# The retention gate's sigmoid, written with ScalarE's exponential and two VectorE operations

## What is computed

```python
h = rms_norm(x, g_mix[l])
proj = h @ w_in[l]
rq, rk, rv, rg, sq, sk, sv, mq = jnp.split(proj, split_at, axis=-1)
...
scores = jnp.einsum('bnihd,bnjhd->bnhij', qc, kc) * intra
...
o = o * lax.rsqrt(jnp.mean(o * o, axis=-1, keepdims=True) + EPS)
o = jax.nn.silu(g.astype(f32)) * o
...
x = x + jnp.concatenate([o_ret, o_swa, o_mem], axis=-1) @ w_out[l]
x = x + moe_ffn(rms_norm(x, g_ffn[l]), ...)
```

## Time and profile before

| | us |
|---|---|
| median of 3 runs | 1069.91 |
| lowest, highest | 1068.23, 1070.17 |
| the profiled execution | 1068.5 |
| its span, first to last instruction | 1066.7 |
| TensorE busy | 983.8 (92%) |
| VectorE busy | 239.5 (22%) |
| ScalarE busy | 131.8 (12%) |
| GpSimd busy | 12.3 (1%) |
| moved by the DMA engines | 424.99 MB, mean 398 GB/s |

### The profile page before, as it was taken

How to read it: one execution, slowest core, us unless ns; L and a number is a source line. 1 busy time by engine, 2 the same in 40 slices (tenths; PEclk the granted TensorE clock), 3 DMA queues, 4 the chain that set the end, 5 groups by cost and what they waited for, 6 DMA issues and landing times.

```text
span 1066.7 us, 11414 instructions
## 1 busy us (share of the span) xinstructions
PE 983.8 (92%) x4524; PEld 402.3 (38%) x4524; DVE 239.5 (22%) x555; ACT 131.8 (12%) x241; POOL 12.3 (1%) x24
## 2 busy tenths in 40 slices
PE   8999999999999998988999898989889998989897
PEld 4446554443434342332424242423324242424233
DVE  0438143030404040211212030402112120304022
ACT  3317110101000000010101000000101000000000
POOL 0200000000000000000000000000000000000000
PEclk9999989999999999999999999999999999999999
DMA  9962869899999999999999999999999999999995
GB/s 374 374 262 87 322 242 413 359 427 429 425 429 425 428 430 426 430 425 430 425 430 426 429 425 430 429 427 429 428 428 428 429 427 429 424 432 426 429 427 243
DMA packets 35427, 424.99 MB, mean 398 GB/s; under 512 B 5040, under 2 KB 5680, under 8 KB 7504
## 3 DMA queue, kind: packets, MB, share of 16 engines
q1 hardware_dynamic: 34592, 423.26, 94.3%
q10 hardware_dynamic: 816, 1.45, 0.4%
HBM read 423.65 MB, written 1.05 MB: 398 GB/s over the span
## 4 chain that ended last, share of the span: by engine, by line
PE 56%; DMA 40%; DVE 1%; ACT 1%; issue 1%; SPq 0%; ACTq 0%
PE psum L1346 21%; DMA ring<-in_w_up 20%; DMA work<-in_w_up 20%; PE psum L1304 15%; PE psum L1226 6%; PE psum L1035 3%; PE psum L1159 3%; PE psum L1002 2%; PE psum L1257 2%; PE psum L1010 2%; PE psum L1027 1%; PE psum L1018 1%; PE psum L1216 0%; ACT work L653 0%; PE psum L1180 0%
## 5 line engine op out<-in xcount | busy, mean ns | idle before, releaser
L1304 PE MATMUL psum<-ring,work 128*64 128x512 f32 x1520 | 344.3, 597 | 48.1 <-DMA ring<-in_w_up 47.5
L1304 PEld LDWEIGHTS psum<-ring,work 128*64 128x64 f32 x1520 | 104.8, 136 | 281.0 <-issue 202.0
L1346 PE MATMUL psum<-ring,work 128*64 128x512 f32 x752 | 165.1, 594 | 5.7 <-ACT work L653 3.1
L1304 PE MATMUL psum<-work 128*64 128x512 f32 x528 | 119.6, 597 | 15.6 <-DMA work<-in_w_up 15.5
L940 DVE TENSOR_TENSOR xy<-psum,xy 128x512 f32<-128x512 f32 x68 | 47.0, 691 | 228.9 <-PE psum L1257 228.9
L1346 PEld LDWEIGHTS psum<-ring,work 128*64 128x64 f32 x752 | 57.7, 137 | 102.6 <-issue 102.6
L646 ACT ACTIVATE work<-work 128x512 f32<-128x512 f32 x32 | 20.2, 630 | 562.3 <-DVE work L970 562.3
L889 DVE TENSOR_SCALAR work<-const 128x128 f32<-128x128 f32 x17 | 4.7, 278 | 353.6 <-PE psum L1216 353.6
L1304 PEld LDWEIGHTS psum<-work 128*64 128x64 f32 x528 | 35.5, 136 | 98.6 <-issue 62.7
L1257 PE MATMUL psum<-work 128*128 128x512 f32 x136 | 67.1, 617 | 1.9 <-issue 1.9
L1226 PE MATMUL psum<-work 128*128 128x128 f32 x544 | 65.1, 278 | 0.0
(11 more groups left out here) (166 smaller groups left out, 420.9 us busy)
## 6 DMA issues: line engine op xcount, KB each, us to landing
ring<-in_w_up SPq DMA_DIRECT2D x95, 2048.0 KB, 32.9
ring<-in_w_down SPq DMA_DIRECT2D x39, 2048.0 KB, 35.3
work<-in_w_up SPq DMA_DIRECT2D x32, 2048.0 KB, 35.0
work<-in_w_down SPq DMA_DIRECT2D x9, 2048.0 KB, 35.3
ring<-in_w_down SPq DMA_DIRECT2D x16, 1024.0 KB, 32.9
work<-in_w_down SPq DMA_DIRECT2D x16, 1024.0 KB, 32.9
ring<-in_w_in SPq DMA_DIRECT2D x3, 2048.0 KB, 27.7
ring<-in_w_out SPq DMA_DIRECT2D x2, 2048.0 KB, 10.3
```

The source lines that it names most:

```text
L1304: mm = pe.matmul(psum[r:r + SLOTS, n], XT[:, j, r:r + SLOTS], weights[e][:, n * N:(n + 1) * N], start=i == 0 and not first, stop=last, ski ...
L1346: mm = pe.matmul(psum[r:r + SLOTS, 4 + n], actT[:, 2 * i + k, r:r + SLOTS], slot[:, (2 * k + e) * D + n * N:(2 * k + e) * D + (n + 1) * N] ...
```

## The change

ScalarE no longer evaluates a sigmoid for the gate but exp(-g), with the factor -rs_x, which VectorE makes once from rs_x. VectorE then adds 1 and takes the reciprocal, in place in rg[:, t], before the product that it made already. The sigmoid of the experts (L646) stays as it is.

```diff
-        ss_x, rs_x = cols(TILES), cols(TILES)
+        ss_x, rs_x, minus_rs_x = cols(TILES), cols(TILES), cols(TILES)
...
             def gate_sigmoid(t):
                 act.wait_ge(rg_done, t + 1)
-                nc.scalar.activation(rg[:, t], psum[:, 3 + t], ACT.Sigmoid, scale=rs_x[:, t:t + 1]).then_inc(rg_sig, 1)
+                nc.scalar.activation(rg[:, t], psum[:, 3 + t], ACT.Exp, scale=minus_rs_x[:, t:t + 1]).then_inc(rg_sig, 1)
...
             dve.wait_ge(rstd["x"], 1)
+            step(V.tensor_scalar(minus_rs_x, rs_x, -1.0, None, ALU.mult))
             for t in range(TILES):
...
             def gate(t):
 
                 dve.wait_ge(rg_sig, t + 1)
+                step(V.tensor_scalar(rg[:, t], rg[:, t], 1.0, None, ALU.add))
+                step(V.reciprocal(rg[:, t], rg[:, t]))
                 V.scalar_tensor_tensor(out=rg[:, t], in0=psum[:, 3 + t], scalar=rs_x[:, t:t + 1], in1=rg[:, t],
                                        op0=ALU.mult, op1=ALU.mult).then_inc(rg_ready, 1)
```

## The result

| | before | changed |
|---|---|---|
| median | 1069.41 us (4 runs) | 1077.97 us (4 runs) |
| lowest to highest | 1068.23 to 1070.17 | 1075.51 to 1078.56 |
| profiled execution, span | 1068.5, 1066.7 | 1078.26, 1076.5 |

The ratio is 1.0079, with a 95% interval of 1.0067 to 1.0091: the changed kernel is slower by 8.6 us, taken between the medians. The forecast was 1076.9 us in a range of 1069.2 to 1080.5. In a later comparison it was 1077.54 against 1068.47 us.

What follows compares the result with a forecast made beforehand. Pace was set by expert weights over the last 700 us, their steady start hanging on TensorE (busy 92%). Chain +5.0 us and clock +2.0 us gave +7.0 us on 1069.9 us: 1076.9 us, range 1069.2 to 1080.5.

Steps and rivals of the forecast that it cites:

- the likeliest case: Whole kernel slower: reciprocal of 2.2 to 3.8 us with a lower clock behind the gap, 1073 to 1079 us; chance 0.35.
- Removed: Four ScalarE table loads of 1.28 us gone, two on the chain: gain 1.29 us at gate 0, 1.13 at gate 1.
- Added and hidden: Negated scale on VectorE at 32 us, one 128x2 instruction of 0.16 us, covered by later idle time: zero cost.
- The reciprocal: On VectorE at both gates over 128x512: 3.2 us each, bounds 0.69 and 6.3; with the addition 3.70 us.
- The sum: Chain through both gates: +2.41 us at gate 0 and +2.57 at gate 1, together +5.0 at TensorE's 97.14.
- The clock: TensorE's clock falls behind 5 us of idle time before the last score: +2.0 us, bounds 0 and 3.4.
- The factor of one: Whatever the mixer's chain gains or loses before 100 us is carried to the end at full size.
- (a): Rival: reciprocal at a column a clock, 0.69 us, so not slower: 1069.8 us; chance 0.27.
- (b): Rival: reciprocal at 8 ns a column, 4.24 us, chain +7.0 us, clock 2.5 us: 1079.4 us; chance 0.20.
- (c): Rival: slow reciprocal, but TensorE's clock holds behind the gap: 1074.9 us; chance 0.12.

Runs made afterwards that it cites:

- the version with tanh: Changed kernel with the gate's sigmoid written as half of 1 + tanh(g/2), no VectorE instruction added on the chain, against the kernel before: 1065.58 us, ratio 0.9976.
- the price experiment: Kernel before plus seven reciprocals over 1 to 512 columns and one 512-column addition on scratch data, off the chain: 1069.15 us, ratio 1.0000.
- the kernel with its clock held up: Changed kernel plus TensorE matmuls between the sliding-window scores and three ahead of the last retention score, results unread: 1073.85 us, ratio 1.0050 against the kernel before.
- the first gate alone: Kernel before with only the first gate tile changed; the second keeps ScalarE's sigmoid and its two table loads: 1071.49 us, ratio 1.0025.
- the other order: Changed kernel with the second half of gate tile 1's projection moved ahead of the sliding-window scores: 1076.23 us; with seven extra matmuls too, 1076.01 us.

## Why the prediction was right

The time lay in the range, 1.1 us above the forecast, and it went the way that the likeliest case said. The loss itself was short by more: forecast +7.0 us, measured +8.6. The forecast had been added to 1069.9 us, and the kernel before measured 1069.4 here and 1068.5 to 1068.8 later, so half a microsecond of the nearness is luck. By the steps of the sum:

- **Removed.** Four loads gone, two of them on the chain. Gate 0: the exponential started when the projection was done and VectorE 0.72 us later, as forecast. The Trainium skill adds a drain of 1.38 us to a load ("ScalarE: Activation LUTs", section "What ACT_TABLE_LOAD costs"). The runs don't agree: the version with tanh starts its gate 0 product 0.72 us after ScalarE gets the tile against 2.01 before, 1.29 us less. ScalarE was idle ahead of that load, but at gate 1 it wasn't, and there the load at 92.75 starts as the instruction ahead of it ends (92.46 + 0.28).
- **Added and hidden.** The negated scale: no sign of it. The seven reciprocals of the price experiment show how large the cover is.
- **The reciprocal.** I took 3.2 us from differences of ten nanoseconds and it is 3.35. The slope of 6 ns a column, taken from the two-column instructions less a fixed 150 ns, is 6.25; the bounds of 0.7 and 6.3 us were both far off. The pair costs 3.83 to 3.85 us with its waits, not 3.70: 0.3 us more in the sum.
- **The sum.** +2.56 at gate 0 (forecast 2.41) and +2.70 at gate 1 (forecast 2.57): 5.3 us, which is what the kernel with its clock held up shows (+5.2).
- **The clock.** Right in kind, too small in size, and half of the place was missing. I forecast a gap of 5 us ahead of the last score and one stretch of lower clock, 98 to 106 us. The rows did not give 5 us but 4.0 (1.44 and the 2.57 of gate 1), and it was 3.14, since the turns ahead of it came late too; the stretch came at 101 to 108. I had noticed nothing at gate 0. There the first memory probabilities come 2.6 us later, TensorE idles for 0.79 us and then runs in short pieces, and the clock fell at 87 us already. That slowed the projection of the second gate tile, and VectorE waited 1.89 us for scores before gate 1. In the first profile the clock's share up to the memory outputs is 1.89 (that wait) + 0.73 (last score and decay) + 1.78 (retention outputs) = 4.4 us; in the second it is 0.28 + 0 + 1.63 = 1.9 us. By the medians it is 3.3 us (8.6 less 5.3), or 3.9 us (what the extra matmuls took off), and the first stretch has no part in it that they show. The forecast had 2.0, bounds 0 and 3.4. The term was mis-sized, by 1.3 to 1.9 us, and that is most of what the sum was short by.
- **The factor of one.** Held as far as single profiles can tell, which is about a microsecond. Counted from the moment at which ScalarE gets the first tile, the first profile is +9.68 us at the memory outputs, +10.6 at the down-projection and +10.8 at the end (9.8 us of span and a start 1.02 earlier); the second is +7.18, +8.14 and +9.8. The 0.9 us that both gain between the memory outputs and the down-projection isn't the change's: the price experiment gains 0.8 there with an unchanged chain, and its stretch of lower clock (138.9 to 149.1 us) is as long as theirs. The further 1.7 us of the second profile comes with its first wait for the weight stream, 32.12 us long against 29.98.
- **The rivals.** (a) fell with the first RECIPROCAL row. (b) had the reciprocal at 4.24 us; its time, 1079.4, was nearly as near as the forecast's, by a reciprocal that is too slow and a clock that costs too little. (c), a clock that holds, is what the experiment with matmuls in both gaps made: 1073.85 us, forecast 1074.9.

Still open: why the first gate alone has a median of only +2.7 us, and what sets the place and length of a stretch of lower clock from one execution to the next. The two profiles of the changed kernel differ by 2.5 us at the memory outputs, and their whole times by 0.2 us. The second one starts its gate 1.1 us later in its span, and waits 1.6 us longer for the first piece of the weight stream (32.12 against 30.52). Whether that wait is tied to the clock or to chance was not followed up, so no single profile gives the price of a stretch in the whole time.

## What to carry to other kernels

Before a function of ScalarE is split into VectorE operations to save a table load, price each operation at the width that it will have: here a load of 1.28 us was traded for a reciprocal of 3.35 us on the same chain. An operation that the trace has only on one or two columns can be priced there, if the fixed part is taken out with the help of other small operations, or run off the chain at several widths. When a wait of TensorE grows, price the clock behind it too, and look at every gap that grows and not only at the longest, though here only the stretch behind the longest one shows in the medians. Take the price of such a stretch from medians, since single profiles of one kernel differed by 2.5 us in it. And look for another function of the same table (here tanh) before an arithmetic way round.

## What the runs showed of the hardware

- The reciprocal on VectorE costs 6.25 ns a column on 128 partitions, from 2 to 512 columns, on a fixed 154 ns (3353 ns for 512); an addition of an immediate over the same 512 columns costs 428 ns.
- The clock's lower level behind idle time of TensorE decided 3 to 4 us of 8.6 (3.3 and 3.9 by two ways). In the changed kernel one stretch of it came behind a gap of 0.79 us with short pieces of work after it, one behind a gap of 3.14 us; in the kernel before, the clock stayed at 1.00 behind one of 1.44 us. Extra matmuls, whose results nobody reads, took 3.9 us off the loss; too many of them, ahead of the last score and with the other order, gained nothing.
- Moving useful work ahead of one gap took it from the next: the clock fell 7 us later and stayed low from 94 to 108 us.
